# Block 2's attention scores from rounded high and low parts on all 128 rows, with the keys going through HBM

## The chip, the cores and the metric

The kernel runs on one core of one Trainium2 chip. The metric is the device time of one launch in microseconds (us). Before the change three runs took 877.80, 877.02 and 877.63 us, median 877.63.

The engines are TensorE (PE, matmuls; PEld is its weight load), VectorE (DVE), ScalarE (ACT), GpSimd (POOL) and SyncE (SP). SP computes nothing here: it issues most of the DMAs, one after the other, and its waits stand in the same line as its DMAs.

## The reference, cut to what matters

Two transformer blocks run one after the other on 256 tokens of width 1024. Block 2 has two attentions over 272 keys (256 tokens and 16 meta tokens): 16 heads that share 4 key heads in a window, and 8 differential heads with two parts each. Queries and keys are turned by their position (`rope`) before they meet:

```python
qa = rope(qa.reshape(B, Lp, SWA_Q_HEADS, HEAD_DIM), pos)      # 16 heads of 64
ka = rope(ka.reshape(B, Lp, SWA_KV_HEADS, HEAD_DIM), pos)     # 4 heads of 64
qb = rope(qb.reshape(B, Lp, DIFF_HEADS, 2, HEAD_DIM), pos)    # 8 heads, two parts
kb = rope(kb.reshape(B, Lp, DIFF_HEADS, 2, HEAD_DIM), pos)
# windowed attention, 16 heads
s_band = jnp.einsum('bqhgd,bkhd->bhgqk', qi, kb).astype(jnp.float32) * scale
# differential attention, 8 heads
s = jnp.einsum('bqhcd,bkhcd->bhcqk', qi, k).astype(jnp.float32) * scale + key_bias
p = jax.nn.softmax(s, axis=-1)
a = (p[:, :, 0] - lam * p[:, :, 1]).astype(v.dtype)
```

Everything is float32, and a head has 64 numbers per token.

## The kernel before

**Weights.** All weights come as 136 blobs of 128 x 2048 floats (1 MB). For each, SP loads `raw` (`load`, L721), ACT writes the rounded high part `whi` (`hi`, L783), DVE writes the rest `wlo` (`lo`, L1742), and PE multiplies with both. A product of two float32 matrices is thus three matmuls of rounded parts (`product`, L495 to L497). In block 2 the blobs go round three places in SBUF. I number the blobs of block 2's first part m = 0 to 33 (`m2` in the code).

**Steps.** The work of this part stands in steps q = 0 to 67, two for each blob: PE multiplies one half of blob q // 2 and then does what `slot(q)` lists. ACT and DVE have loops over the same q, with their own lists. Each engine works strictly in the order in which this is written, and only semaphores hold one back for another.

**Blobs.** Blobs 0 to 4 make keys, 5 and 8 to 11 values, 6, 7 and 12 to 17 queries. Then come gates and up-projections, the windowed ones (18 to 29, both kinds) before the differential ones (30 to 33 are the differential up-projection).

**A key blob.** PE writes it to a pair of PSUM banks; two pairs alternate, so blob m waits until blob m - 2 has been copied out (`wait_pair_free`, semaphores `taken_a` and `taken_d`). ACT copies it to `kraw` (`keys_out`, L1008); there are two of these too, so `keys_out(i)` first waits until key blob i - 2 has been turned (semaphore `kt_ok`). SP copies the halves of the heads across partitions to `kswap` with four DMAs (`swap_halves`, L759). DVE turns them: two products and a sum (`turned_keys`, L2231 to L2240), written straight to `ksT` and `kbT`. On DVE's list these turns stand ahead of the `lo` of a later blob. A query blob goes the same way (`queries_low` L1017, `queries_raw` L2212, `turned_queries` L2220 to L2224, into `qsT` and `qbT`); a value blob is copied out by ACT (`values_out`, L1026), turned over by PE (L1611) and copied again by ACT (`values_in`, L1035 to L1042).

**Units.** From step 22 on there is one unit for each step, 32 in all: two heads (or the two parts of one) for 128 tokens. PE computes its scores at the end of step 22 + U (L1639): one float32 matmul for each head, on 64 rows of the array, the first head on the upper 64 rows and the second on the lower 64. DVE takes the maximum (`unit_front`, L1941), ACT the exponentials (L1065), DVE the sums (`unit_back`), ACT scales (L1097), and two steps later PE transposes the result and multiplies it with the values. The scores of unit U wait for the maximum of unit U - 1 (`u_max`).

Of the kernel before, what the change touches and what calls it, by code (L numbers as in the profile page):

```python
# [18 lines left out]
F32 = mybir.dt.float32  # L19
# [5 lines left out]
P = 128  # L25
# [85 lines left out]
QUERIES = (6, 7, 12, 13, 14, 15, 16, 17)  # L111
# [3 lines left out]
VALUES_AT = {12: 0, 18: 1, 20: 2, 22: 3, 24: 4}  # L115
# [7 lines left out]
def values_blob(i):  # L123

    return 7 + i if i else 5
# [7 lines left out]
def unit_place(U):  # L133

    return U % S_UNITS // 8 * 4 + U % 4, U % 8 // 4


def query_made(U):

    cc, _ = unit_place(U)  # L140
    return 6 + U // S_UNITS * 4 + cc // 2
# [23 lines left out]
def build(nc, w, x, meta, consts, turns, rows, grow, out):  # L165

    with ExitStack() as ctx:
# [143 lines left out]
        o_tok = [at("o_tok0", [P, P], F32, dead + KC * TOK), new("o_tok1", [P, P]), new("o_tok2", [P, P])]  # L311
# [135 lines left out]
        def link(eng, name, ins):  # L447
# [12 lines left out]
            "aaaaa" + "a" + "dd" + "aaaa" + "dd" + "dddd" + "dddd" + "dd" + "dd")  # L460
# [255 lines left out]
        def _(sp):  # L716
# [58 lines left out]
        def _(act):  # L775
# [242 lines left out]

            def values_out(i):
# [25 lines left out]
            for q in range(2 * OUT2):  # L1045
# [221 lines left out]
        def _(pe):  # L1267
# [333 lines left out]
            def slot(q):  # L1601
# [26 lines left out]
                if 0 <= U < UNITS:  # L1628
                    cc, t = unit_place(U)
                    pe.wait_ge(kt_ok, query_made(U))  # L1630
# [4 lines left out]
                    qT = qsT if U < S_UNITS else qbT  # L1635
# [953 lines left out]
```

## Time and profile before

| | |
|---|---|
| median of three runs | 877.63 us |
| the profiled execution, and its span | 877.45 us, 875.6 us |
| PE busy | 868.0 us, 99% of the span, 4820 matmuls |
| DVE, ACT, POOL busy | 623.7 us (71%), 459.2 us (52%), 46.2 us (5%) |
| chain that ended last | PE 99% |
| DMA | 156.75 MB, mean 179 GB/s |

The profile is one execution. Of the 877.45 us the span covers 875.6, and 1.85 lie around it. Busy time of PE runs to the modelled end of each matmul, so that short pauses do not show as idle; the distance from the start of one matmul to the start of the next tells more. Block 2's first part lies between 396 and 655 us of the span, its key blobs between 396 and 427 us, and its units between 468 and 628 us.

### The profile page before, as it was taken

To read this page: it belongs to the slowest core of one execution; us is meant where nothing else is said; L and a number is where in the kernel's file an instruction comes from. 1 tells how busy PE (TensorE), PEld (TensorE's weight loads), DVE (VectorE), ACT (ScalarE), POOL (GpSimd) and SP (SyncE) were. 2 spreads that over 40 slices of the span, in tenths; PEclk is the share of its full clock that TensorE was granted. 3 is DMA by queue.
4 is the path that set the end of the run, shared out by engine and by line. 5 is a ranking of instruction groups with operands and counts; after the bars stand their busy time and mean duration, and the time that the engine had idled before them with its cause. 6 is when DMAs were issued, how large, how long until landed. Compare 5 with 4: busy or idle time off the path is not lost.

```text
span 875.6 us, 13035 instructions
## 1 busy us (share of the span) xinstructions
PE 868.0 (99%) x4820; PEld 731.3 (84%) x4820; DVE 623.7 (71%) x987; ACT 459.2 (52%) x735; POOL 46.2 (5%) x83
## 2 busy tenths in 40 slices
PE   9999999999999999999999999999999999999997
PEld 6887788888888888889998777777888888888886
DVE  6867777765876666668855888787766876666665
ACT  6546534334644444454556777677643654444443
POOL 1000010000200000002000000132300100000000
PEclk9999999999999999999999999999999999999999
DMA  9955344553565555353683335323274365555541
GB/s 328 412 207 187 129 160 144 192 192 144 190 242 190 189 195 188 142 190 104 207 300 106 123 123 170 145 100 142 97 265 175 119 228 189 183 192 192 186 143 48
DMA packets 26830, 156.75 MB, mean 179 GB/s; under 512 B 3600, under 2 KB 5136, under 8 KB 9376
## 3 DMA queue, kind: packets, MB, share of 16 engines
q1 hardware_dynamic: 24048, 148.71, 47.6%
q10 hardware_dynamic: 2736, 7.42, 2.4%
q8 instruction: 29, 0.48, 0.2%
q14 instruction: 17, 0.14, 0.0%
HBM read 151.45 MB, written 1.05 MB: 174 GB/s over the span
## 4 chain that ended last, share of the span: by engine, by line
PE 99%; DMA 0%; DVE 0%; DVEq 0%; SPq 0%; ACTq 0%; ACT 0%; issue 0%
PE ps L495 19%; PE ps L497 18%; PE ps L496 18%; PE ps L661 8%; PE ps L646 8%; PE ps L665 4%; PE ps L642 4%; PE ps L674 4%; PE ps L1639 2%; PE ps L676 2%; PE ps L530 1%; PE ps L1574 1%; PE ps L1598 1%; PE ps L1593 1%; PE ps L1588 1%; PE ps L1283 1%
## 5 line engine op out<-in xcount | busy, mean ns | idle before, releaser
L1742 DVE TENSOR_TENSOR wlo<-raw,whi 128x2048 fp32r<-128x2048 f32 x134 | 306.7, 2290 | 151.7 <-ACT whi L783 151.4
L783 ACT ACTIVATE whi<-raw 128x2048 fp32r<-128x2048 f32 x134 | 256.4, 1914 | 182.8 <-PE ps L497 110.8
L495 PE MATMUL ps<-whi,xT 128*128 128x512 f32 x192 | 76.8, 400 | 0.0
L497 PE MATMUL ps<-whi,xT 128*128 128x512 f32 x192 | 75.0, 391 | 0.0
L496 PE MATMUL ps<-wlo,xT 128*128 128x512 f32 x192 | 74.8, 390 | 0.0
L495 PE MATMUL ps<-whi,fT_h 128*128 128x512 f32 x128 | 50.2, 392 | 0.0
L496 PE MATMUL ps<-wlo,fT_h 128*128 128x512 f32 x128 | 49.8, 389 | 0.0
L497 PE MATMUL ps<-whi,fT_l 128*128 128x512 f32 x128 | 49.8, 389 | 0.0
L495 PE MATMUL ps<-x_all,whi 128*128 128x272 f32 x160 | 46.6, 291 | 0.0
L496 PE MATMUL ps<-x_all,whi 128*128 128x272 f32 x160 | 46.2, 289 | 0.0
L497 PE MATMUL ps<-x_all,wlo 128*128 128x272 f32 x160 | 46.2, 289 | 0.0
L497 PEld LDWEIGHTS ps<-whi,xT 128*128 128x128 f32 x192 | 36.0, 188 | 7.8
L1065 ACT ACTIVATE sc<-sc,usoft 128x272 f32<-128x272 f32 x64 | 32.7, 512 | 18.7 <-DVE usoft L1950 14.0
L495 PEld LDWEIGHTS ps<-whi,xT 128*128 128x128 f32 x192 | 36.1, 188 | 7.4
L646 PE MATMUL ps<-x_all,whi 128*128 128x512 f32 x176 | 42.0, 391 | 0.0
L496 PEld LDWEIGHTS ps<-wlo,xT 128*128 128x128 f32 x192 | 36.1, 188 | 7.0
L495 PE MATMUL ps<-whi,x_all 128*128 128x512 f32 x96 | 39.4, 410 | 0.0
L661 PE MATMUL ps<-x_all,whi 128*128 128x512 f32 x160 | 38.0, 390 | 0.0
L1224 POOL TENSOR_TENSOR stat<-stat,cst 128x1 f32<-128x1 f32 x10 | 11.9, 1204 | 490.0 <-DVE stat L1762 260.9
L646 PEld LDWEIGHTS ps<-x_all,whi 128*128 128x128 f32 x176 | 32.3, 188 | 6.3
L497 PE MATMUL ps<-whi,x_all 128*128 128x512 f32 x96 | 37.5, 391 | 0.0
L496 PE MATMUL ps<-wlo,x_all 128*128 128x512 f32 x96 | 37.4, 390 | 0.0
(347 smaller groups left out, 1834.5 us busy)
## 6 DMA issues: line engine op xcount, KB each, us to landing
raw<-weights SPq DMA_DIRECT2D x134, 1024.0 KB, 4.8
kswap<-kraw SPq DMA_DIRECT2D x52, 68.0 KB, 2.0
cst<-consts SPq DMA_DIRECT2D x1, 1371.0 KB, 13.0
raw<-weights SPq DMA_DIRECT2D x4, 256.0 KB, 5.5
raw<-weights SPq DMA_DIRECT2D x2, 512.0 KB, 7.2
gate_a<-gain_rows ACTq DMA_DIRECT2D x2, 512.0 KB, 7.7
gate_r<-gain_rows ACTq DMA_DIRECT2D x2, 512.0 KB, 6.7
gate_s<-gain_rows ACTq DMA_DIRECT2D x2, 512.0 KB, 6.6
```

The lines of the kernel that those rows point to most:

```text
L495: pe.matmul(o, lh, rh, start=first, stop=False)
L496: pe.matmul(o, lh, rl, start=False, stop=False)
L497: return pe.matmul(o, ll, rh, start=False, stop=last)
L642: pe.matmul(ps[:, bank0 + j, 0:TOK], vl[:, k, j * P:(j + 1) * P], x[:, 0, k, :], start=k == 0, stop=False, skip_group_check=True)
L646: m = pe.matmul(ps[:, bank0 + j, :], vh[:, k, j * P:(j + 1) * P], x[:, :, k, :], start=False, stop=k == KC - 1, skip_group_check=True)
L661: pe.matmul(ps[:, bank0 + j, :], vh[:, k, j * P:(j + 1) * P], x[:, :, k, :], start=k == 0, stop=False)
L665: m = pe.matmul(ps[:, bank0 + j, 0:TOK], vl[:, k, j * P:(j + 1) * P], x[:, 0, k, :], start=False, stop=k == KC - 1)
L674: pe.matmul(ps[:, bank + j, :], vh[:, k, j * P:(j + 1) * P], x2[:, :, k, :], start=k == 0, stop=False)
L676: m = pe.matmul(ps[:, bank + j, 0:TOK], vl[:, k, j * P:(j + 1) * P], x2[:, 0, k, :], start=False, stop=k == KC - 1)
L783: act.activation(whi[s][:], raw[s][:], ACT.Copy).then_inc(split_hi, 1)
L1065: ins = act.activation(scores(U, u), scores(U, u), ACT.Exp, bias=st[:, 2, u:u + 1], accum_out=st[:, 4, u:u + 1])
L1742: dve.tensor_tensor(wlo[s][:], raw[s][:], whi[s][:], ALU.subtract).then_inc(split_lo, 1)
```

## The change

The scores are computed from rounded parts as well. Queries and keys are each split into high (rounded) and low part. For one head the query's high part stands on 64 rows of the array and its low part on the other 64 (`qs`, `qd`), and the key comes in two forms, the high part on all 128 rows and the low part on all 128 rows (`kB`). Two matmuls of 128 rows then give (high + low) times high and (high + low) times low. A unit has four of them instead of two float32 ones.

To make the parts, ACT writes the high part and DVE the rest: `keys_high`, `keys_rest` for five key blobs, `queries_high`, `queries_rest` for eight query blobs. To bring the parts to their rows, SP stores the keys' parts in HBM (`store_keys`, 5 DMAs) and reads them back twice over into a ring of two chunks (`load_shared_keys`, 12 DMAs; `load_keys`, 8 times 4), and copies the queries' parts inside SBUF (`store_queries`, 8 times 4). `kt_ok` now counts the rests and no longer the turns; the turns have the new semaphore `rot_ok`. `keys_out(i)` waits for `kt_ok` as before.

Blobs are reordered: queries are 6, 7, 9, 10, 12, 13, 15, 17 and values 5, 8, 11, 14, 16; the windowed up-projection moves from 26 to 29 to 22 to 25. The two loads of gate rows on ACT move from steps 13 and 40 to steps 38 and 54, and the gates' steps on DVE and ACT with the blobs.

```diff
-QUERIES = (6, 7, 12, 13, 14, 15, 16, 17)
+QUERIES = (6, 7, 9, 10, 12, 13, 15, 17)
+QUERY_PLACE = (0, 1, 4, 2, 3, 5, 6, 7)
+VALUES = (5, 8, 11, 14, 16)
-VALUES_AT = {12: 0, 18: 1, 20: 2, 22: 3, 24: 4}
+VALUES_AT = {12: 0, 18: 1, 24: 2, 30: 3, 34: 4}
...
+            def store_keys(i):
+
+                sp.wait_ge(kt_ok, i + 1)
+                sp.dma_start(kd[i], knat[i % 2][:].bitcast(F32)).then_inc(kd_out[i % 2], 16)
+
+            def load_shared_keys(r):
+
+                if r == 0:
+                    sp.wait_ge(kd_out[0], 16 * 3)
+                    sp.wait_ge(kd_out[1], 16 * 2)
+                for copy in range(2):
+                    o = slice(copy * DH, (copy + 1) * DH)
+                    sp.dma_start(kB[r][o, 0:2, 0:KEYS], kd[0, 0:DH, :, r, :]).then_inc(kb_in[r], 16)
+                    sp.dma_start(kB[r][o, 2:4, N_META:KEYS], kd[0, DH:P, :, r, 0:TOK]).then_inc(kb_in[r], 16)
+                    sp.dma_start(kB[r][o, 2:4, 0:N_META], kd[0, DH:P, :, r, TOK:KEYS]).then_inc(kb_in[r], 16)
+
+            def load_keys(cc):
+
+                sp.wait_ge(u_sc, 2 * cc + 14 if cc else 8)
+                for u in range(2):
+                    for copy in range(2):
+                        sp.dma_start(kB[cc % 2][copy * DH:(copy + 1) * DH, 2 * u:2 * u + 2, 0:KEYS],
+                                     kd[1 + cc // 2, u * DH:(u + 1) * DH, :, cc % 2, :]).then_inc(kb_in[cc % 2], 16)
+
+            def store_queries(m2):
+
+                i = QUERIES.index(m2)
+                sp.wait_ge(kt_ok, 5 + i + 1)
...
+                sp.dma_start(dst[0][low, both, :], hi[low].bitcast(F32)).then_inc(q_in[j], 16)
+                sp.dma_start(dst[0][high, both, :], lo[low].bitcast(F32)).then_inc(q_in[j], 16)
+                sp.dma_start(dst[1][low, both, :], lo[high].bitcast(F32)).then_inc(q_in[j], 16)
+                sp.dma_start(dst[1][high, both, :], hi[high].bitcast(F32)).then_inc(q_in[j], 16)
+
-            plain = N1 + 24
+            plain = N1 + 30
             for n in range(N1, plain):
                 load(n, w[n], n - 2)
-                if n - N1 - 4 in SWAPPED:
-                    swap_halves(n - N1 - 4)
+                m = n - N1
+                if 7 <= m < 12:
+                    store_keys(m - 7)
+                if m in (12, 13):
+                    load_shared_keys(m - 12)
+                if m == 19:
+                    load_keys(0)
+                if 22 <= m < 29:
+                    load_keys(m - 21)
+                if m - 6 in QUERIES:
+                    store_queries(m - 6)
+                if m - 4 in SWAPPED:
+                    swap_halves(m - 4)
...
+            def keys_high(i):
+
+                act.wait_ge(rot_ok, i + 1)
+                if i >= 2:
+
+                    act.wait_ge(kd_out[i % 2], 16 * (i // 2))
+                act.activation(knat[i % 2][:, 0], kraw[i % 2][:], ACT.Copy).then_inc(rot_hi, 1)
+
+            def queries_high(m2):
+
+                i = QUERIES.index(m2)
+                act.wait_ge(rot_ok, 5 + i + 1)
+                if i >= 2:
+
+                    act.wait_ge(q_in[QUERY_PLACE[i - 2]], 64)
+                act.activation(qh[i % 2][:], kraw[m2 % 2][:, :, 0:TOK], ACT.Copy).then_inc(rot_hi, 1)
...
+                if q in (4, 6, 8, 10, 12):
+                    keys_high(q // 2 - 2)
+                if q % 2 == 1 and (q - 5) // 2 in QUERIES:
+                    queries_high((q - 5) // 2)
...
                 if 0 <= U < UNITS:
                     cc, t = unit_place(U)
-                    pe.wait_ge(kt_ok, query_made(U))
+                    if t == 0:
+                        pe.wait_ge(q_in[query_of(U)], 64)
+                        pe.wait_ge(kb_in[key_slot(U)], keys_loaded(U))
...
                     for u in range(2):
-                        half = slice(u * DH, (u + 1) * DH)
-                        kT = ksT[half, cc // 4, :] if U < S_UNITS else kbT[half, cc, :]
-                        m = pe.matmul(ps[:, 4 + u, 0:KEYS], qT[half, cc, t * P:(t + 1) * P], kT, start=True, stop=True)
+                        for v in range(2):
+                            m = pe.matmul(ps[:, 4 + u, 0:KEYS], qT[u][:, cc, t * P:(t + 1) * P].bitcast(F32R),
+                                          kT[:, 2 * u + v, 0:KEYS].bitcast(F32R), start=v == 0, stop=v == 1)
...
+            def queries_rest(m2):
+
+                i = QUERIES.index(m2)
+                dve.wait_ge(rot_hi, 5 + i + 1)
+                dve.tensor_tensor(ql[i % 2][:], kraw[m2 % 2][:, :, 0:TOK], qh[i % 2][:], ALU.subtract).then_inc(kt_ok, 1)
+
+            def keys_rest(i):
+
+                dve.wait_ge(rot_hi, i + 1)
+                dve.tensor_tensor(knat[i % 2][:, 1], kraw[i % 2][:], knat[i % 2][:, 0], ALU.subtract).then_inc(kt_ok, 1)
...
-                if i == 0:
-                    dve.tensor_tensor(ksT[0:DH], kraw[b][0:DH], kswap[b][0:DH], ALU.add)
...
-                m.then_inc(kt_ok, 1)
+                dve.tensor_tensor(kraw[b][:], kraw[b][:], kswap[b][:], ALU.add).then_inc(rot_ok, 1)
...
+                if q in (5, 7, 9, 11, 13):
+                    keys_rest((q - 5) // 2)
...
+                if q % 2 == 1 and (q - 5) // 2 in QUERIES:
+                    queries_rest((q - 5) // 2)
```

**ACT, from `keys_out(1)` in step 4 on.** Before; the number behind a name is the buffer's, `whi2` is the high part of blob 4 and `whi3` that of blob 5:

```order
L1008 ACTIVATE kraw1_118<-ps 128x272 x2
L783 ACTIVATE whi2_56<-raw2_55 128x2048
L1008 ACTIVATE kraw0_117<-ps 128x272 x2
L783 ACTIVATE whi3_59<-raw3_58 128x2048
L1008 ACTIVATE kraw1_118<-ps 128x272 x2
```

The same place of ACT in the changed kernel (`knat` holds a key blob's two parts):

```order
L1085 ACTIVATE kraw1_118<-ps 128x272 x2
L1102 ACTIVATE knat0_121<-kraw0_117 128x544
L860 ACTIVATE whi2_56<-raw2_55 128x2048
L1085 ACTIVATE kraw0_117<-ps 128x272 x2
L1102 ACTIVATE knat1_122<-kraw1_118 128x544
L860 ACTIVATE whi3_59<-raw3_58 128x2048
L1085 ACTIVATE kraw1_118<-ps 128x272 x2
```

A `keys_high` has come between each `keys_out` and the `hi` behind it, and it needs a turn that DVE has to finish.

**DVE, from `turned_keys(0)` in step 4 on.** Before; `wlo2` belongs to blob 4, `wlo3` to blob 5:

```order
L2231 TENSOR_TENSOR kraw0_117<-kraw0_117,turn_142 128x544
L2232 TENSOR_TENSOR kswap0_119<-kswap0_119,turn_142 128x544
L2234 TENSOR_TENSOR ksT_122<-kraw0_117,kswap0_119 64x544
L2235 TENSOR_TENSOR ksT_122<-kraw0_117,kswap0_119 64x2x256
L2237 TENSOR_TENSOR ksT_122<-kraw0_117,kswap0_119 64x2x16
L1742 TENSOR_TENSOR wlo2_57<-raw2_55,whi2_56 128x2048
L2231 TENSOR_TENSOR kraw1_118<-kraw1_118,turn_142 128x544
L2232 TENSOR_TENSOR kswap1_120<-kswap1_120,turn_142 128x544
L2240 TENSOR_TENSOR kbT_121<-kraw1_118,kswap1_120 128x544
```

The same place of DVE in the changed kernel:

```order
L2343 TENSOR_TENSOR kraw0_117<-kraw0_117,turn_149 128x544
L2344 TENSOR_TENSOR kswap0_119<-kswap0_119,turn_149 128x544
L2345 TENSOR_TENSOR kraw0_117<-kraw0_117,kswap0_119 128x544
L1844 TENSOR_TENSOR wlo2_57<-raw2_55,whi2_56 128x2048
L2343 TENSOR_TENSOR kraw1_118<-kraw1_118,turn_149 128x544
L2344 TENSOR_TENSOR kswap1_120<-kswap1_120,turn_149 128x544
L2345 TENSOR_TENSOR kraw1_118<-kraw1_118,kswap1_120 128x544
L2336 TENSOR_TENSOR knat0_121<-kraw0_117,knat0_121 128x544
```

`kt_ok` was raised for key blob 0 ahead of `wlo2` and is now raised behind the turn of key blob 1, by the rest (L2336).

**SP, from the load of blob 13 (`raw2`) to the swap of blob 10.** Before, the same stretch, blobs 12 to 16, had loads and one swap alone:

```order
L721 DMA raw1_52<-weights 128x2048
L721 DMA raw2_55<-weights 128x2048
L721 DMA raw3_58<-weights 128x2048
L721 DMA raw1_52<-weights 128x2048
L721 DMA raw2_55<-weights 128x2048
L759 DMA kswap0_119<-kraw0_117 32x544 x4
```

In the changed kernel, from the load of blob 13 on; `key_parts` is the HBM scratch:

```order
L750 DMA raw2_55<-weights 128x2048
L802 DMA kB1_124<-key_parts 64x2x272
L803 DMA kB1_124<-key_parts 64x2x256
L804 DMA kB1_124<-key_parts 64x2x16
L802 DMA kB1_124<-key_parts 64x2x272
L803 DMA kB1_124<-key_parts 64x2x256
L804 DMA kB1_124<-key_parts 64x2x16
L822 DMA qs0_137<-qh1_135 64x512
L823 DMA qs0_137<-ql1_153 64x512
L824 DMA qs1_138<-ql1_153 64x512
L825 DMA qs1_138<-qh1_135 64x512
L788 DMA kswap1_120<-kraw1_118 32x544 x4
```

The swap of blob 9 (the last row) stands behind ten new DMAs, and the ten of blob 12 stand ahead of those.

## Rows read from the trace of the kernel before

**Rows 1.** The page: busy time of the engines, and the chain by engine.

```profile
PE 868.0 (99%) x4820; PEld 731.3 (84%) x4820; DVE 623.7 (71%) x987; ACT 459.2 (52%) x735; POOL 46.2 (5%) x83
...
PE 99%; DMA 0%; DVE 0%; DVEq 0%; SPq 0%; ACTq 0%; ACT 0%; issue 0%
```

**Rows 2.** Timeline of PE at the scores of units 3 and 22: start, length, work.

```profile
481.54 0.73 PE L1639 MATMUL ps<-ksT,qsT 64*128 64x272 f32 x4
482.20 0.50 PE L674 MATMUL ps<-x_all,whi 128*128 128x512 f32 x1
...
574.45 0.27 PE L1577 MATMUL ps<-cst,sc 128*32 128x128 f32 x1
574.56 0.27 PE L1626 MATMUL ps<-cst,o_tok 128*128 128x128 f32 x1
574.76 0.73 PE L1639 MATMUL ps<-kbT,qbT 64*128 64x272 f32 x4
```

**Rows 3.** Timeline of PE in key blob 0: matmuls of rounded parts.

```profile
396.00 0.29 PE L496 MATMUL ps<-x_all,whi 128*128 128x272 f32 x1
396.13 0.29 PE L497 MATMUL ps<-x_all,wlo 128*128 128x272 f32 x1
```

**Rows 4.** Timeline of ACT, steps 4 to 14; in brackets idle time and its releaser.

```profile
408.55 0.69 ACT L1008 ACTIVATE kraw<-ps 128x272 f32<-128x272 f32 x2 [1.77 <-PE ps L497]
409.12 1.92 ACT L783 ACTIVATE whi<-raw 128x2048 fp32r<-128x2048 f32 x1
416.92 0.69 ACT L1008 ACTIVATE kraw<-ps 128x272 f32<-128x272 f32 x2 [5.88 <-DVE ksT L2237]
...
421.27 0.69 ACT L1008 ACTIVATE kraw<-ps 128x272 f32<-128x272 f32 x2 [1.86 <-DVE kbT L2240]
...
426.97 0.69 ACT L1008 ACTIVATE kraw<-ps 128x272 f32<-128x272 f32 x2 [3.21 <-PE ps L497]
...
433.05 0.62 ACT L1026 ACTIVATE kraw<-ps 128x544 f32<-128x544 f32 x1 [3.59 <-PE ps L497]
...
437.07 0.84 ACT L1042 ACTIVATE vs<-ps,stat 128x256 f32<-128x256 f32 x2
439.31 0.60 ACT L1017 ACTIVATE kraw<-ps 128x512 f32<-128x512 f32 x1 [1.40 <-PE ps L676]
```

**Rows 5.** Timeline of DVE, steps 4 to 11.

```profile
415.31 0.72 DVE L2234 TENSOR_TENSOR ksT<-kraw,kswap 64x544 f32<-64x544 f32 x1
...
416.86 2.29 DVE L1742 TENSOR_TENSOR wlo<-raw,whi 128x2048 fp32r<-128x2048 f32 x1
...
421.54 0.72 DVE L2231 TENSOR_TENSOR kraw<-kraw,turn 128x544 f32<-128x544 f32 x1 [0.36 <-DMA kswap<-kraw]
...
426.69 0.73 DVE L2231 TENSOR_TENSOR kraw<-kraw,turn 128x544 f32<-128x544 f32 x1 [0.82 <-DMA kswap<-kraw]
...
432.01 0.73 DVE L2231 TENSOR_TENSOR kraw<-kraw,turn 128x544 f32<-128x544 f32 x1 [0.99 <-DMA kswap<-kraw]
```

**Rows 6.** SP's timeline, one swap; all swaps' issue in ns; their landing.

```profile
417.63 2.41 SPq L759 DMA_DIRECT2D kswap<-kraw  x4
...
L759 SPq DMA_DIRECT2D kswap<-kraw x52: 507/591/1482, 403.2 to 538.4; - x52
...
DMA to landing us min/median/max: 1.9/2.0/3.9
```

**Rows 7.** Timelines: DVE at unit 0's scores, PE and DVE at unit 15's.

```profile
468.59 0.44 DVE L1941 CUSTOM_DVE_ANT_0 sc<-ps,cst 128x272 f32<-128x272 f32 x1 [6.26 <-PE ps L1639]
...
541.48 0.73 PE L1639 MATMUL ps<-ksT,qsT 64*128 64x272 f32 x4
...
543.91 0.43 DVE L1941 CUSTOM_DVE_ANT_0 sc<-ps,cst 128x272 f32<-128x272 f32 x1
```

**Rows 8.** Windows: length, busy PE, PEld, DVE, ACT, POOL; clock, DMA share, GB/s.

```profile
500.00:540.00 40.00, 40.00 (x291) 31.04 (x290) 35.79 (x100) 28.65 (x80) 0.00 (x0) 1.00 0.38 125
...
870.00:875.60 5.60, 0.00 (x0) 0.00 (x0) 2.69 (x5) 0.70 (x2) 0.55 (x1) 0.67 0.50 187
```

More of the change, by code:

```diff
@@ L123, in values_blob @@
 def values_blob(i):
-    return 7 + i if i else 5
+    return VALUES[i]
 def swaps_before(m2):
@@ L133, in unit_place, with query_of, key_slot, keys_loaded @@
 def unit_place(U):
-    return U % S_UNITS // 8 * 4 + U % 4, U % 8 // 4
-def query_made(U):
+    return U % S_UNITS // 2, U % 2
+def query_of(U):
     cc, _ = unit_place(U)
-    return 6 + U // S_UNITS * 4 + cc // 2
+    return U // S_UNITS * 4 + cc // 2
+def key_slot(U):
+    cc, _ = unit_place(U)
+    return cc // 4 if U < S_UNITS else cc % 2
+def keys_loaded(U):
+    cc, _ = unit_place(U)
+    return 96 if U < S_UNITS else 96 + 64 * (cc // 2 + 1)
 def slot_of(n):
@@ L285, in build @@
         kswap = [new("kswap0", [P, 2, KEYS]), new("kswap1", [P, 2, KEYS])]
-        kbT = new("kbT", [P, F_HEADS, KEYS])
-        ksT = new("ksT", [P, S_KV // 2, KEYS])
+        keys_at = top[0]
+        knat = [new("knat0", [P, 2, 2, KEYS], F32R), new("knat1", [P, 2, 2, KEYS], F32R)]
+        top[0] = keys_at
+        kB = [new("kB0", [P, 4, XSTEP]), new("kB1", [P, 4, XSTEP])]
         vs_meta = new("vs_meta", [P, S_KV * DH])
         o_junk = new("o_junk", [P, P])
-        rrow2 = new("rrow2", [P, TOK])
+        rrow2 = at("rrow2", [P, TOK], F32, top[0])
+        qh = [new("qh0", [P, 2, TOK], F32R)]
+        ql = [new("ql0", [P, 2, TOK], F32R)]
         assert top[0] <= 3 * BLOB
@@ L409, in build @@
         v_ps = sem("v_ps")
+        rot_ok = sem("rot_ok")
+        rot_hi = sem("rot_hi")
         kt_ok = sem("kt_ok")
+        kd_out = [sem("kd_out0"), sem("kd_out1")]
+        kb_in = [sem("kb_in0"), sem("kb_in1")]
+        q_in = [sem(f"q_in{j}") for j in range(len(QUERIES))]
         ql_ok = sem("ql_ok")
@@ new lines, in load_keys @@
+            def load_keys(cc):
[7 more added lines that the diff above has]
+                sp.wait_ge(kt_ok, 5 + i + 1)
+                j = QUERY_PLACE[i]
+                both = slice(2 * (j % 4), 2 * (j % 4) + 2)
+                hi, lo, dst = qh[i % 2], ql[i % 2], qs if j < 4 else qd
+                low, high = slice(0, DH), slice(DH, P)
+                sp.dma_start(dst[0][low, both, :], hi[low].bitcast(F32)).then_inc(q_in[j], 16)
+                sp.dma_start(dst[0][high, both, :], lo[low].bitcast(F32)).then_inc(q_in[j], 16)
+                sp.dma_start(dst[1][low, both, :], lo[high].bitcast(F32)).then_inc(q_in[j], 16)
+                sp.dma_start(dst[1][high, both, :], hi[high].bitcast(F32)).then_inc(q_in[j], 16)
@@ L2481, in weight_stream @@
     out += blob_tokens(w, at[2], 256)
-    for q in range(2):
-        out += blob_tokens(qa, 256 * q, 256)
-    for q in range(4):
-        out += blob_tokens(w, at[5] + 256 * q, 256)
-    for q in range(2, 4):
-        out += blob_tokens(qa, 256 * q, 256)
-    for q in range(4):
-        out += blob_tokens(w, at[3] + 256 * q, 256)
-    for q in range(4):
-        out += blob_tokens(w, at[6] + BANK * q)
-    for up in (head_pairs(np.asarray(i["w_branch_swa_2"])[0], 0, 0), np.asarray(i["w_branch_diff_2"])[0]):
+    values = 0
+    for m2 in range(6, 18):
+        if m2 in QUERIES:
+            j = QUERY_PLACE[QUERIES.index(m2)]
+            out += blob_tokens(qa, 256 * j, 256) if j < 4 else blob_tokens(w, at[3] + 256 * (j - 4), 256)
+        else:
+            out += blob_tokens(w, at[5] + 256 * values, 256)
+            values += 1
+    for g, up in enumerate((head_pairs(np.asarray(i["w_branch_swa_2"])[0], 0, 0), np.asarray(i["w_branch_diff_2"])[0])):
+        for q in range(2):
+            out += blob_tokens(w, at[6] + BANK * (2 * g + q))
         out += blob_tokens(up, 0) + blob_tokens(up, BANK)
```

50 lines of the change are left out of this document (25 added, 25 removed).

## The prediction, made before the changed kernel ran

> **What bounds the kernel now.** I read the page first: PE is busy for 99% of the span and the chain that ended last is 99% PE [rows 1], so whatever PE does not have to do is time saved, and whatever makes PE wait is time lost in full. Next I read PE's timeline at a unit's scores, for the price of what is removed [rows 2, 3]. Then the timelines of ACT, DVE and SP over the key blobs, because that is where the change adds waits: the reader is to see there how early each result is that PE needs [rows 4 to 6]. Last come the units, where DVE has the least spare time [rows 7, 8].
>
> Two kinds of lead matter. Around the key blobs ACT's copy of key blob 2 waited 5.88 us for DVE and was done at 416.92 + 0.69 = 417.6 [rows 4]; PE needed that bank for blob 4. Blob 4 ended at 426.97 and blob 1 at 408.55 [rows 4], 6.1 us for each, so blob 4 began at 420.8. The lead was 3.2 us. The low part of blob 4 was ready at 416.86 + 2.29 = 419.1 [rows 5], a lead of 1.7.
>
> **What the change saves.** Before, the four records of one unit's scores take PE from 481.54 to 482.20, 0.66 us [rows 2]. Matmuls of rounded parts with 272 columns start 0.125 us apart [rows 3] (two starts show 0.13 by rounding; I take 0.125), so the four new ones need 0.50: 0.16 saved in each of the 32 units. In the 16 differential units a step goes too: their scores come 0.20 behind the transpose ahead of them, where two transposes stand 0.11 apart [rows 2]. The new matmuls use all 128 rows as the transposes do, so I count 0.09 more for each. The windowed units come behind matmuls of 64 columns, and I count nothing there. Sum: 32 x 0.16 + 16 x 0.09 = 6.6 us. Bounds: 3.4 if a pause of 0.1 stays behind the scores in all units, 8.0 if all 32 lose the 0.09. I take 6.6, the value that changes only what rows 2 show.
>
> The Trainium skill (TensorEngine Tiling, Key Properties) says that changing the tiling mode, though not merely the tile, drains the engine. By that rule the windowed units, whose neighbours use another mode than full size, keep their pause, and the saving is 6.6; without it, with the 0.09 a matter of float32 alone, it would be 8.0. The 0.20 against 0.11 agrees with the rule and does not prove it.
>
> **The key blobs, where the new waits are.** The new ACT copy is priced as ACT's 128x544 copy, 0.6 (L1026 [rows 4]), the new DVE subtraction as a 544-wide sum, 0.7 [rows 5]; a turn is three of these, 2.1. Both have the shapes of the new work, only their sources differ. I follow the chain in the span's time.
>
> Step 4 and 5: the turn of key 0 ends at 415.31 + 0.7 = 416.0. ACT, free since 409.2, now stands at `keys_high(0)` and not at the high part of blob 4, so that part is made from 416.65 to 418.6 instead of 409.1 to 411.0. DVE then does the low part of blob 4 (to 420.85), the turn of key 1 (2.1, to 422.95) and only then the rest of key 0 (to 423.65). This raises `kt_ok`, for which `keys_out(2)` waits: copied out at 424.35 instead of 417.6. PE waits for the bank from 420.7: **3.65 us**.
>
> Step 7: from a copied key to its turn, SP's four issues (2.41) and the landing (2.0) [rows 6], it took 3.9, 4.7 and 4.35 us (417.6 to 421.54, 421.96 to 426.69, 427.66 to 432.01 [rows 4, 5]); I take 4.3. Turn of key 2 from 428.65 to 430.75, rest of key 1 to 431.4, low part of blob 5 to 433.65. PE ends blob 4 at 424.35 + 6.1 = 430.45: **3.2 us**.
>
> Step 9: `keys_out(3)` to 432.05, turn 436.35 to 438.45, rest of key 2 to 439.1, low part of blob 6 to 441.35. PE ends blob 5 at 439.75: **1.6 us**.
>
> Step 11 and 12: `keys_out(4)` to 439.8, turn 444.1 to 446.2, rest of key 3 to 446.85. `values_out(0)` needs this buffer, so the values are out at 447.45. PE comes to their transposes after half of blob 6. That blob took 433.05 to 439.31 [rows 4] with six transposes at 0.11, so 2.8 for a half: 444.15, **3.3 us**.
>
> Step 13: ACT goes on with `keys_high(4)`, a high part of 1.92 and the two kinds of value copies (0.84 for L1042 [rows 4] and an estimated 0.5 for the small one), to 451.4; PE would want that bank at 450.95: **0.45 us**.
>
> Sum 12.2 us. Blob 6 then ends at 451 instead of 439.3 (L1017 [rows 4]). With 3.9 or 4.7 for the swaps, three of which are on this chain, it is 11.0 or 13.4. `keys_high(2)` also waits until the store of key 0 has landed. No row shows a store to HBM; it is issued at about 427.5 and has until 437.8. Below, it costs nothing; above, if it took three times the slowest swap's landing (11.7 us [rows 6]), 1.4. I take 0. Past blob 7 DVE has no more key turns on its list and catches up.
>
> **SP's queue.** A DMA costs SP about 0.6 us (2.41 for four [rows 6]), and the change adds 81, 49 us of SP time. Most of it has cover, since the weights are loaded well ahead. At one place it has none: the swap of blob 9 stands behind 22 issues in SP's turns for blobs 12 and 13, 13 us. SP comes to the load of blob 12 at 461.7, after the swap of blob 7 (DVE reaches that query at 459.3: behind the low part of blob 7 at 449.1 stand two more low parts, each behind its high part, and two sums), and waits to 463.5 for the last store. Ten issues, a load and ten more put the swap at 476.2 to 478.6, landed at 480.5. The turn of blob 9 stands ahead of unit 0's maximum on DVE: 480.5 + 2.0 + 1.0 = 483.5. PE, from 451.4 on, does three query blobs (5.6), a value blob (6.1), transposes (0.65) and half of blob 11 (3.0), has these scores done at 478.5, and wants the maximum for the next at 481.6: 1.9 us. ACT's copy for the next values waits for the rest of blob 9 as well, another 0.8. I take 2.7. Bounds: with the quickest issue, 0.51 [rows 6], the swap is 1.8 earlier and 0.9 stays; at 0.7 it is 5.
>
> **DVE in the units.** In steps 28 to 37 DVE falls behind: at unit 0 it waits for the scores, at unit 15 it starts 543.91 - 541.48 = 2.4 us after PE began them [rows 7], and it is busy 35.79 of 40 us [rows 8]. The change makes PE's step 0.16 shorter there and adds a subtraction of about 0.6 for each query blob, but spreads the queries: 4.8 instead of 6 of them between steps 24 and 39, 4.8 x 3.1 us against 6 x 2.5 (a sum, a turn, and now the rest; estimates from rows 5), equal work in 16 x 0.16 = 2.5 us less. Before, no wait came of it; now it starts without a lead, as just worked out. I take 1.5, bounds 0 and 4 (the 2.5 and as much as one step of its 2.4 lag gives back). The gates' steps move with their blobs at the same distance and cost nothing; key and query reads (3 steps, 13 us ahead of use) neither.
>
> **Sum.** -6.6 + 12.2 + 2.7 + 1.5 = +9.8 us. The profiled execution took 877.45, which gives 887.3; it lies 0.2 below the median, so about 887.5.
>
> **The rivals.**
> 1. The new waits fit into the leads, and only the saving is left: 877.6 - 6.6 = 871. For it: the waits of ACT's copies for DVE shrink by themselves, 5.88, 1.86, and the third waits for PE instead [rows 4]. Against it: leads of 3.2 and 1.7 us stand against delays of 6.7 and 1.8. The point from which it decides is 6.6 us of stall: if the `kt_ok` of key 0 came before 420, half of the chain would be gone. A mixture can also end near zero.
> 2. SP becomes the bound: if the 20 new issues ahead of the swap of blob 9 cost 1.0 each, between the median 0.59 and the slowest 1.48 [rows 6], it comes 8 us later and PE waits for all of it: 895.5. For it: the new ones have twice as many rows and pieces. Against it: the median.
> 3. PE's clock falls in the stalls. It is granted in full throughout, and at 0.67 on average in the last 5.6 us, where PE has nothing to do [rows 8]: a stretch at the lower level of 1.2 GHz after PE went idle. An average of 0.67 means that some 3.7 of the 5.6 us were at half. If each of the three stalls over 3 us led to as much, with PE at work in it, it would add 3 x 1.9 = 5.6 us: 893. The Trainium skill (TensorE: Matmul & The Clock Gate, HAM oscillation) says that idle gaps between bursts throttle PE again.
>
> **How the numbers follow.** Forecast 0.70, and its own range is 883 to 892; rival 1 0.10, a mixture near zero 0.04, rival 2 0.10, rival 3 0.06. The range of 881 to 895 holds the forecast with both ends of the swaps, of SP and of DVE, and most of rivals 2 and 3, and leaves out rival 1. Under 0.2% (1.75 us) no difference can be told. Faster 0.10, same 0.04, slower 0.86.
>
> **What would show it.** In the profile after, the scores' line takes four matmuls 0.125 apart. PE has idle time, for which the page names DVE's low parts, ACT's copies of keys and values: five pauses of 3.65, 3.2, 1.6, 3.3 and 0.45 us before 452. `keys_out(2)` starts at about 423.7. Unit 0's maximum waits for a swap. I am wrong if PE reaches blob 7 before 445, or if the pauses are there but between 455 and 620 us PE loses more than 8 us.

## The result, and the profile after

The changed kernel takes 891.83 us (median of four runs, 890.81 to 892.91) against 877.33 for the kernel before, measured beside it. The ratio is 1.0166, with a 95% interval of 1.0148 to 1.0184: slower by 14.5 us. The prediction said 887.5, with a range of 881 to 895. The profiled execution after has a span of 890.7 us against 875.6.

The page after, engines and the chain by engine; it answers to [rows 1]:

```profile
PE 868.0 (97%) x4820; PEld 743.6 (83%) x4820; DVE 630.6 (71%) x998; ACT 464.8 (52%) x748; POOL 46.8 (5%) x83
...
PE 88%; DVE 3%; SPq 3%; DMA 3%; ACT 1%; issue 1%; POOL 1%; DVEq 0%; ACTq 0%
```

PE has the same number of matmul records and the same busy time, and the second is chance: with the new scores alone (run 1 below) it is busy for 859.4 us, and most of what lies between that and 868.0 is work at half clock. PE is no longer busy for 99% of the span but for 97%. The chain's share, 88% PE against 99%, says that there are waits and not what they cost: in run 8, which beats both kernels, it is 86%. The waits of PE say where they are (what PE waited for: us in total, times, longest; `usoft` holds the unit's maximum, `kraw` the copies of keys and values, `vs` the values as the units use them, `wlo` a low part of weights):

```profile
PE ps L1740 <- DVE usoft L2050: 4.9, 1, 4.9
PE ps L1711 <- ACT kraw L1120: 3.7, 1, 3.7
PE ps L524 <- ACT kraw L1085: 3.6, 1, 3.6
PE ps L1414 <- DVE kaT L2070: 1.4, 1, 1.4
PE ps L703 <- ACT vs L1136: 1.3, 1, 1.3
PE ps L703 <- DVE wlo L1844: 1.2, 1, 1.2
```

The fourth stands at the start of the kernel, before as after. The other five are new: scores of unit 1 (L1740), transposes of the first values (L1711), blob 4 (L524), blobs 7 and 6 (L703). PE's timeline shows the same, here at blob 4, blob 6, the end of blob 6's first half, blob 7 and unit 1:

```profile
423.66 0.56 PE L524 MATMUL ps<-x_all,whi 128*128 128x272 f32 x1 [3.58 <-ACT kraw L1085]
424.02 0.43 PE L525 MATMUL ps<-x_all,whi 128*128 128x272 f32 x1
424.25 0.43 PE L526 MATMUL ps<-x_all,wlo 128*128 128x272 f32 x1
...
439.89 2.11 PE L703 MATMUL ps<-x_all,whi 128*128 128x512 f32 x8 [1.16 <-DVE wlo L1844]
...
446.70 0.69 PE L1711 MATMUL ps<-cst,kraw 128*128 128x128 f32 x2 [3.75 <-ACT kraw L1120]
...
453.17 1.16 PE L703 MATMUL ps<-x_all,whi 128*128 128x512 f32 x4 [1.32 <-ACT vs L1136]
...
488.26 1.05 PE L1740 MATMUL ps<-kB,qs 128*128 128x272 f32 x3 [4.89 <-DVE usoft L2050]
```

Look at the second and third row too: behind the pause matmuls of 272 columns start 0.23 us apart, where [rows 3] has 0.125. The windows (length, busy PE, PEld, DVE, ACT, POOL; granted clock, DMA share, GB/s) show the reason: three stretches at 0.50, the lower level of 1.2 GHz, with PE at work in them.

```profile
422.60:429.40 6.80, 5.74 (x25) 5.77 (x26) 2.06 (x4) 3.02 (x4) 0.00 (x0) 0.50 0.46 106
429.40:446.50 17.10, 12.39 (x89) 11.45 (x87) 11.22 (x13) 6.78 (x9) 0.00 (x0) 1.00 0.79 246
446.50:449.90 3.40, 3.20 (x11) 2.67 (x12) 1.63 (x1) 0.76 (x3) 0.00 (x0) 0.50 0.74 239
...
487.40:494.20 6.80, 5.94 (x19) 5.18 (x20) 6.59 (x19) 4.24 (x14) 0.00 (x0) 0.50 0.79 269
494.20:640.00 145.80, 145.80 (x1012) 126.31 (x1010) 120.49 (x347) 107.94 (x303) 20.33 (x42) 1.00 0.60 187
```

**The key blobs.** ACT's timeline after, which answers to [rows 4]:

```profile
415.29 0.66 ACT L1102 ACTIVATE knat<-kraw 128x544 fp32r<-128x544 f32 x1 [6.82 <-DVE kraw L2345]
415.85 1.90 ACT L860 ACTIVATE whi<-raw 128x2048 fp32r<-128x2048 f32 x1
422.83 0.69 ACT L1085 ACTIVATE kraw<-ps 128x272 f32<-128x272 f32 x2 [5.08 <-DVE knat L2336]
...
430.29 0.69 ACT L1085 ACTIVATE kraw<-ps 128x272 f32<-128x272 f32 x2 [4.43 <-DVE knat L2336]
433.49 0.66 ACT L1102 ACTIVATE knat<-kraw 128x544 fp32r<-128x544 f32 x1 [2.52 <-DMA key_parts<-knat]
437.73 0.69 ACT L1085 ACTIVATE kraw<-ps 128x272 f32<-128x272 f32 x2 [1.77 <-DVE knat L2336]
440.93 0.66 ACT L1102 ACTIVATE knat<-kraw 128x544 fp32r<-128x544 f32 x1 [2.52 <-DMA key_parts<-knat]
...
446.02 0.62 ACT L1120 ACTIVATE kraw<-ps 128x544 f32<-128x544 f32 x1 [2.63 <-DVE knat L2336]
449.29 0.66 ACT L1102 ACTIVATE knat<-kraw 128x544 fp32r<-128x544 f32 x1 [2.64 <-DMA key_parts<-knat]
449.85 1.90 ACT L860 ACTIVATE whi<-raw 128x2048 fp32r<-128x2048 f32 x1
...
452.19 0.84 ACT L1136 ACTIVATE vs<-ps,stat 128x256 f32<-128x256 f32 x2
```

The chain starts in the first row: ACT stands 6.82 us at `keys_high(0)`, and the high part of blob 4, made at 409.12 in [rows 4], comes at 415.85. `keys_out(2)` starts at 422.83 instead of 416.92. The chain goes round through `keys_out`, SP's swap, DVE's turn and rest, and back to the next `keys_out`. Three times ACT also stands 2.5 to 2.6 us until the store of an earlier key blob has landed. The third time, at 449.29, a high part and the values' copies stand behind it, and PE's blob 7 (453.17) waits for the last of these copies.

From the page, DMA issues (us from issue to landing last):

```profile
raw<-weights SPq DMA_DIRECT2D x134, 1024.0 KB, 4.8
kB<-key_parts SPq DMA_DIRECT2D x36, 136.0 KB, 3.4
kswap<-kraw SPq DMA_DIRECT2D x52, 68.0 KB, 2.1
key_parts<-knat SPq DMA_DIRECT2D x5, 544.0 KB, 6.9
```

**Units 0 and 1.** SP (see [rows 6]), then DVE (see [rows 7]):

```profile
466.49 0.57 SPq L802 DMA_DIRECT2D kB<-key_parts  x1
...
480.23 0.60 SPq L825 DMA_DIRECT2D qs<-qh  x1
480.87 2.49 SPq L788 DMA_DIRECT2D kswap<-kraw  x4
```

```profile
485.07 0.69 DVE L2322 TENSOR_TENSOR kraw<-kraw,turn 128x512 f32<-128x512 f32 x1 [6.64 <-DMA kswap<-kraw]
...
487.01 0.43 DVE L2043 CUSTOM_DVE_ANT_0 sc<-ps,cst 128x272 f32<-128x272 f32 x1
```

The swap of blob 9 stands behind 21 issues, DVE waits 6.64 us for it ahead of unit 0's maximum, and PE's scores of unit 1 wait for that.

**The balance.** The first key blob starts 0.77 us earlier in the trace after (395.11 against 395.88), and up to the end of blob 3 this stays so. It isn't gained by the change: the distance is there after the first 9 us, in which both kernels do the same, and over the ten profiled executions of this document that start lies between 395.10 and 396.23. Counted from there, the end of blob 8 comes 14.9 us later, and the end of the kernel 15.8. Blobs 0 to 8 have the same content in both kernels, so 14.9 is the loss at the key blobs. From there to the end another 0.9 is lost: the pause of 5.05 and its stretch at half speed, less what the scores save.

### The profile page after: what moved, and what is told of

It is laid out like the page before. It is cut to its first block, busy times and chain, and to the rows that moved or that the text cites. A ratio compares the mean times of both kernels' runs of the same rounds, so it can differ in the third digit from the quotient of the medians.

```text
span 890.7 us, 13143 instructions
## 1 busy us (share of the span) xinstructions
PE 868.0 (97%) x4820; PEld 743.6 (83%) x4820; DVE 630.6 (71%) x998; ACT 464.8 (52%) x748; POOL 46.8 (5%) x83
## 4 chain that ended last, share of the span: by engine, by line
PE 88%; DVE 3%; SPq 3%; DMA 3%; ACT 1%; issue 1%; POOL 1%; DVEq 0%; ACTq 0%
PE ps L524 16%; PE ps L526 16%; PE ps L525 16%; PE ps L690 8%; PE ps L675 7%; PE ps L694 4%; PE ps L671 4%; PE ps L1740 2%; PE ps L703 2%; DMA key_parts<-knat 2%; PE ps L559 1%; SPq L788 1%; PE ps L1674 1%; PE ps L705 1%; PE ps L1698 1%
## 5 line engine op out<-in xcount | busy, mean ns | idle before, releaser
L524 PE MATMUL ps<-whi,xT 128*128 128x512 f32 x192 | 76.9, 400 | 0.0
L524 PE MATMUL ps<-x_all,whi 128*128 128x272 f32 x160 | 47.8, 299 | 3.6 <-ACT kraw L1085 3.6
L524 PE MATMUL ps<-whi,fT_h 128*128 128x512 f32 x128 | 50.3, 393 | 0.0
L525 PE MATMUL ps<-x_all,whi 128*128 128x272 f32 x160 | 47.3, 296 | 0.0
L524 PEld LDWEIGHTS ps<-whi,xT 128*128 128x128 f32 x192 | 36.1, 188 | 7.3
L524 PE MATMUL ps<-whi,x_all 128*128 128x512 f32 x96 | 38.2, 398 | 0.0
```

The lines of the kernel that those rows point to most:

```text
L524: pe.matmul(o, lh, rh, start=first, stop=False)
L525: pe.matmul(o, lh, rl, start=False, stop=False)
```

## The experiments

Each is a change to the kernel after, except the first. Ratios are to the kernel before, run beside it.

**1. The scores alone, in the kernel before.** Instead of the two float32 matmuls of a unit, four rounded ones on 128 rows, straight from the kernel's queries and keys; without the parts, so the scores are other numbers. The four tiles of queries and keys are declared as rounded (not shown).

```diff
+                    kT = ksT[:, cc // 4, :] if U < S_UNITS else kbT[:, cc, :]
                     for u in range(2):
-                        half = slice(u * DH, (u + 1) * DH)
-                        kT = ksT[half, cc // 4, :] if U < S_UNITS else kbT[half, cc, :]
-                        m = pe.matmul(ps[:, 4 + u, 0:KEYS], qT[half, cc, t * P:(t + 1) * P], kT, start=True, stop=True)
+                        for v in range(2):
+                            m = pe.matmul(ps[:, 4 + u, 0:KEYS], qT[:, cc, t * P:(t + 1) * P],
+                                          kT, start=v == 0, stop=v == 1)
```

> The kernel before with one thing changed: a unit's scores are four matmuls of rounded numbers on all 128 rows in place of two float32 ones on 64 rows each; no parts are made or moved, so the scores are not those of the reference. It prices the saving alone. My forecast priced it at 6.6 us (0.16 in each of 32 units, 0.09 more in the differential ones). The profile of the changed kernel suggests more: its undisturbed steps are 0.17 us shorter in the windowed units (5.00 to 4.83) and 0.36 in the differential ones (4.70 to 4.34), 8.5 us in all. By the first 870.7 us, by the second 868.8; the rival, that the saving was an effect of the reordered blobs, says 877.3.

870.52 us, ratio 0.9928 (0.9912 to 0.9945): 6.4 us saved. The forecast's 6.6 stands.

**2. Everything but the scores' form.** The kernel after with float32 scores on 64 rows, from the high parts alone.

```diff
-                        for v in range(2):
-                            m = pe.matmul(ps[:, 4 + u, 0:KEYS], qT[u][:, cc, t * P:(t + 1) * P].bitcast(F32R),
-                                          kT[:, 2 * u + v, 0:KEYS].bitcast(F32R), start=v == 0, stop=v == 1)
+                        half = slice(u * DH, (u + 1) * DH)
+                        m = pe.matmul(ps[:, 4 + u, 0:KEYS], qT[u][half, cc, t * P:(t + 1) * P],
+                                      kT[half, 2 * u, 0:KEYS], start=True, stop=True)
```

> The changed kernel with the scores computed as before, two float32 matmuls on 64 rows each, from the high parts alone (the low parts are made and moved but not used, so the scores are less exact). All making and moving of parts stays. It prices everything but the saving. If the loss lies in the making and moving, it is 8 us slower than the changed kernel, about 900, and shows the same pauses: some 3.6, 1.2, 3.7 and 1.3 us over the key blobs and nearly 5 at unit 1. If part of the loss came from the new scores themselves (reads of the ring, DVE too late because PE's steps are shorter), it is less than 8 slower, 895 or so.

899.26 us, ratio 1.0246 (1.0225 to 1.0266): 7.4 us above the kernel after, with the same pauses in the trace (3.86, 1.44, 4.16 and 4.37 us). From unit 2's scores to unit 31's, where neither kernel has a long pause, it takes 142.7 us for 136.3, 6.5 more. The saving is in the changed kernel too, and the loss is in what surrounds the scores.

**3. The key blobs in another order.** All the same work. ACT makes the high part of the weights ahead of `keys_high`, DVE makes the rest ahead of the next turn, SP's stores come one blob earlier.

```diff
# ACT, step q
-                if q in (4, 6, 8, 10, 12):
-                    keys_high(q // 2 - 2)
+                if q == 13:
+                    keys_high(4)
...
                     hi(N1 + m + 2)
+                if q in (4, 6, 8, 10):
+                    keys_high(q // 2 - 2)
...
# DVE: rest, lo, turn in the place of lo, turn, rest (in step 5 lo, rest, turn)
...
# SP
-                if 7 <= m < 12:
-                    store_keys(m - 7)
+                if 6 <= m < 11:
+                    store_keys(m - 6)
```

> The changed kernel with another order over the key blobs: ACT makes the weights' high part ahead of keys_high (the last keys_high goes behind the value copies), DVE makes a key's rest, and the next low part, ahead of the next key's turn, and SP stores a key one blob earlier, ahead of the next swap. No operation is taken away. If the pauses over the key blobs come from the places of these in their lists, kt_ok of key 0 comes at about 418.5 instead of 422.7, and of the 14.6 us lost between blob 3 and blob 7 at most 1 is left, with the clock at its upper level there: 877 to 880, with unit 1's pause still in it. If it is the amount of new work on ACT and DVE, or the landing of the stores (6.9 us each), that counts, most of the loss stays: 888 or more.

878.42 us (ten runs, 876.09 to 881.64), ratio 1.0017 (1.0004 to 1.0029): 13.4 us come back. The loss at the key blobs is order and not work. Three places changed at once, on ACT, DVE and SP, and no run tells what each is worth. PE's waits in this run:

```profile
PE ps L1742 <- DVE usoft L2052: 6.7, 1, 6.7
...
PE ps L1713 <- ACT kraw L1120: 0.8, 2, 0.4
```

The key blobs' waits shrank to 0.8 us, and the wait at unit 1 grew from 4.9 to 6.7: PE arrives earlier, and SP's row of issues is as long as it was. The profiled execution took 881.01, 2.6 us above this run's median, so the 6.7 may be more than the usual wait.

**4. The first swap ahead.** SP issues the swap of blob 9 ahead of the second block of key loads.

```diff
+                if m == 13:
+                    swap_halves(9)
...
-                if m - 4 in SWAPPED:
+                if m - 4 in SWAPPED and m != 13:
```

> The changed kernel with one swap moved: SP issues the swap of query blob 9 behind the load of blob 13, ahead of the six reads of keys and the four copies of query parts that stood before it. If unit 1's pause of 4.9 us is the SP queue ahead of that swap, the pause goes, the fall of the clock with it: 7 us less, 884.5 to 885.5. If DVE's own work is late there, or the copies only move the wait to the query parts, at most 2 us are gained: 890.

891.73 us, ratio 1.0162 (1.0145 to 1.0179): nothing. Unit 1's pause is gone, and one step later PE waits as long:

```profile
PE ps L1676 <- ACT sc L1197: 4.6, 1, 4.6
PE ps L1713 <- ACT kraw L1122: 3.8, 2, 3.7
```

The swap of blob 10 now stands behind the ten issues (it starts at 486.13), and DVE's turn of that blob stands ahead of unit 1's sums. My expectation missed this second swap.

**5. No swap behind the long row.** As in 4 (only the first ten issues and the load go ahead), and the second block of key loads two blobs later.

```diff
-                if m in (12, 13):
-                    load_shared_keys(m - 12)
+                if m in (12, 15):
+                    load_shared_keys((m - 12) // 3)
```

> The changed kernel with the second block of ten shared key loads issued by SP two blobs later (at blob 15 in the place of 13), and the swap of query blob 9 ahead of the store of queries in the same step. All swaps of queries then stand in front of SP's long block. With only the first swap put ahead, the pause had moved from unit 0's turn to unit 1's, behind the same ten issues. Theory (SP's 20 issues of 0.6 us in a row are what makes the units late): no pause over 1 us at unit 0, 1 or 2, no half clock between 480 and 500 us, and 4.9 us of pause with 2 to 2.5 us of clock come back: 884.5 to 885.5. Rival 1 (DVE's order at the first units costs a pause of its own): 1 to 5 us stay, 886 to 890. Rival 2 (the later block delays keys of later units): a new pause between 500 and 530 us, 890 or more.

887.56 us, ratio 1.0113 (1.0098 to 1.0129): 4.3 us back. Unit 1's pause is 1.9 us instead of 5.2, and the clock stays at 1.00 there:

```profile
480.00:500.00 20.00, 18.00 (x135) 15.72 (x133) 16.17 (x44) 14.09 (x34) 0.00 (x0) 1.00 0.91 253
```

The time lies in rival 1's range, and its reason does not show: the long row made the units late, and the 1.8 us of pause that stay come from the swap itself. DVE's turn of blob 9 waits for it and starts at 481.96, 3.5 us behind the end of the swap's issues, where it took 2.0 in run 4; why this swap landed late is open. The rest of what is missing to the 7 I expected is that with the clock up two smaller pauses of 0.65 and 0.85 us appear at 488 and 518 (L1713, ACT's copy of values), as in run 6.

**6. PE kept busy in two pauses.** Matmuls without use, 13 ahead of blob 4 and 20 ahead of unit 1's scores; the waits stay.

```diff
+            def filler(count):
+                for k in range(count):
+                    pe.matmul(ps[:, 6, :], x2_h[:, k % KC, 0:P], x_all[:, 0, 0:2, 0:TOK], start=True, stop=True)
```

> The changed kernel with matmuls that serve no result (512 columns, into a bank of their own) in PE's two longest pauses: 13 before blob 4, 20 before unit 1's scores. What PE waits for stays the same; only PE is busy meanwhile. Theory (the granted clock falls because PE stood idle, and the stretch at half speed behind the pause costs time of its own): the granted clock stays at its upper level at 422 and 487 us; blob 4 takes 6.1 us again in the place of 8.85, of which the wait behind it takes some back; behind unit 1's pause 2.5 to 3 us come back for good; 888 to 890. Rival 1 (the clock cost nothing that the waits would not have cost): 891.8. Rival 2 (the clock falls for another reason): it falls here too, 891.8 or more.

892.62 us, ratio 1.0173 (1.0159 to 1.0187): no gain, although the clock did what the theory says. Windows at blob 4, at the unfilled pause of blob 6, and behind unit 1's:

```profile
424.40:430.40 6.00, 6.00 (x48) 6.00 (x48) 2.18 (x4) 2.18 (x2) 0.00 (x0) 1.00 0.55 134
...
448.90:452.30 3.40, 3.40 (x12) 2.71 (x10) 1.08 (x2) 2.06 (x2) 0.00 (x0) 0.50 0.52 155
...
489.40:496.00 6.60, 6.18 (x39) 5.47 (x40) 6.43 (x16) 4.36 (x15) 0.00 (x0) 1.00 0.93 287
```

The clock stays up where PE was kept busy and falls at the pause that was not filled. But the time is not there to be had, as PE's waits show:

```profile
PE ps L1711 <- ACT kraw L1120: 5.0, 3, 4.1
PE ps L524 <- DVE wlo L1853: 2.6, 1, 2.6
```

Blob 4 takes 6.1 us again, and then PE waits 2.6 for the low part of blob 5. The pause that I had forecast at 3.2 was there all along: in the kernel after, blob 4 at half speed filled it (8.8 us for the blob). At unit 1, 2.0 us are won by the end of blob 12, and by blob 20 PE has waited 1.7 of them away for DVE and ACT in the units. The other runs agree at blob 4: from its first matmul to blob 5's it is 8.80 or 8.81 us in the kernel after and in runs 2, 4, 5, 6 and 7, with 6.8, 3.4 or no us of it at half clock. The unfilled pause of blob 6 has no such run, but a comparison: in run 2 the clock stays at 0.50 there to 453.1, in the kernel after to 449.9, and blob 7 starts 6.45 and 6.47 us behind the end of the pause. Blob 7 waits for ACT's copies either way. Rival 1 stands: the clock's fall cost almost nothing that the waits would not have cost.

**7. Five key buffers.** No `keys_high` waits for a store.

```diff
-                if i >= 2:
-
-                    act.wait_ge(kd_out[i % 2], 16 * (i // 2))
-                act.activation(knat[i % 2][:, 0], kraw[i % 2][:], ACT.Copy).then_inc(rot_hi, 1)
+                act.activation(knat[i][:, 0], kraw[i % 2][:], ACT.Copy).then_inc(rot_hi, 1)
...
```

> The changed kernel with five natural-key buffers in the place of two (three more tiles of float32, in the place of the scores' float32 tiles), so that keys_high of a step never waits for the 544 KB store that read the buffer before it. In the changed kernel keys_high stood 2.5 to 2.6 us three times for such a landing, and 2.1 us of the pause before blob 6 came out of that. Theory (the landing is a link in the chain before blobs 4, 6 and 8): the three waits go, the chain ACT - DVE - swap stays as it is, 1.5 to 3 us come back, 889 to 890.5. Rival (the landing is hidden behind the swap and DVE's turns, which are late anyway): 891.8, no change.

890.90 us, ratio 1.0155 (1.0141 to 1.0169). By the medians this is 0.9 us, less than the intervals can tell. The trace is clearer: ACT's three waits for a landing are gone, and with them PE's pause of 1.5 us ahead of blob 7. ACT's timeline at that place:

```profile
447.05 0.65 ACT L1102 ACTIVATE knat<-kraw 128x544 fp32r<-128x544 f32 x1
...
449.94 0.84 ACT L1136 ACTIVATE vs<-ps,stat 128x256 f32<-128x256 f32 x2
```

The values' copies start 2.25 us earlier than after, where they stood behind `keys_high(4)`. The pauses before blobs 4 and 6 are as they were: there the landing was hidden behind the swap. I had placed its effect at blob 6; it was at blob 7. There the landing and the slow stretch stand for each other: without the landing the copies are done at 450.8, and PE, at half clock, comes to blob 7 only at 452.27.

**8. The orders of 3 and 5 and the buffers of 7 together.**

> The three orders together: ACT's high parts ahead of the copies of keys and DVE's low parts ahead of the next turn (as in the run with the key order), SP's stores one blob earlier, five natural-key buffers, and SP's second block of shared keys at blob 15 behind the queries' swaps. All of the change's arithmetic stays. Theory (the change's loss is all order, and its matmuls are worth what the scores alone gave, 6.4 us): no pause of PE over 1 us anywhere between 415 and 530 us, clock at its upper level throughout, 870 to 872, faster than both kernels. Rival 1 (DVE's and ACT's added work costs something in the units also without a pause): 873 to 876. Rival 2 (the pause at unit 1 moves once more): 875 to 880.

872.66 us (872.27 to 873.07), ratio 0.9948 (0.9935 to 0.9962): faster than both kernels, by 4.5 us than before, and 19.2 faster than the kernel after, where runs 3, 5 and 7 gave 13.4, 4.3 and 0.9 one by one. PE's waits and the clock over the stretch in question:

```profile
PE ps L1715 <- ACT kraw L1122: 1.8, 4, 0.6
```

```profile
415.00:530.00 115.00, 113.13 (x845) 102.62 (x845) 93.48 (x197) 77.78 (x166) 0.00 (x0) 1.00 0.75 233
```

Four pauses are left, of 0.62 to 0.90 us from one matmul to the next (434.7, 453.2, 473.0, 502.8). It lands 0.7 above my range, and 2.1 above the scores alone: about 1.3 from the two pauses in the units, 0.5 from the key blobs, 0.4 between blobs 36 and 38. That is rival 1 in small: ACT's copies of values stand behind the scaling of a unit or the rest of a query.

## Why the prediction was right, and where its sizes were off

The direction, the places and the mechanism held: nearly all loss is in waits that the new order makes, first at the key blobs, then at SP's queue. The time is 4.3 us above the forecast and inside the range. A part of that closeness is luck: 1.5 us were added for DVE in the units, a wait that this trace doesn't have, and they cover a part of what the other terms lack. Term by term, by the traces:

| term | forecast | measured |
|---|---|---|
| scores | -6.6 | -6.6, as what the other rows leave of the sum (run 1 alone: -6.4) |
| key blobs | +12.2 | +14.9 |
| SP's queue, unit 1 | +2.7 | +5.05, and 2.1 of clock behind it |
| DVE in the units | +1.5 | 0 beside the clock's 2.1; 1.3 without it (run 8) |
| blobs 36 to 38 | 0 | +0.4 |
| sum | +9.8 | +15.8 from blob 3 on; 15.1 between the spans, since the trace after starts 0.77 ahead |

- **Scores.** The sum was right and its parts were not. A unit of before has three costs: 0.20 ahead, 0.66, and a first matmul behind it that takes 0.34 to the next instead of 0.22. [rows 2] shows that last as a length of 0.50; I didn't count it. After, a differential unit:

```profile
596.47 0.27 PE L1726 MATMUL ps<-cst,o_tok 128*128 128x128 f32 x1
596.50 0.75 PE L1740 MATMUL ps<-kB,qd 128*128 128x272 f32 x4
597.09 0.39 PE L524 MATMUL ps<-whi,sT_h 128*128 128x512 f32 x1
597.31 0.39 PE L525 MATMUL ps<-wlo,sT_h 128*128 128x512 f32 x1
```

  0.03 + 0.59 + 0.22 instead of 0.20 + 0.66 + 0.34: 0.36 saved, forecast 0.25. In the windowed units the 0.20 stays, the block takes 0.61, and 0.17 is saved: 0.05 in it and 0.12 behind it. The gross is 16 x 0.36 + 16 x 0.17 = 8.5. Some 2 us of it are not there: the steps behind the scores of units 16 and 17 are only 0.13 and 0.14 shorter than before and that behind unit 29 is not, and in run 1 there are three pauses of 0.5 to 0.7 us at 532, 542 and 552. The Trainium skill (TensorEngine Tiling, Key Properties) has a change of tiling mode drain the engine. The trace agrees: behind matmuls of 64 columns the new scores still come 0.20 later, behind full ones 0.03.
- **Key blobs.** Forecast pauses 3.65, 3.2, 1.6, 3.3, 0.45. Measured, less the usual step: 3.75; none, but blob 4 longer by 2.75 at half speed in its place; 1.3; 3.9; and in the place of the 0.45 a pause of 1.5 ahead of blob 7, behind a half blob 6 that took 5.0 us with its transposes at half clock, where run 8 has 3.5. That is 14.7, and the rest of the 14.9 is spread over the steps. The first four are right within 0.6 each, and their errors cancel. The size that was wrong is blob 7's: 3.0 for 0.45. Its term is the landing of the stores, taken as 0 with an upper end of 1.4. A store landed after 6.9 us, against the 2.0 of a swap, from whose rows I bounded it; `keys_high(4)` waits 2.64 for it, and the values' copies behind it are done at 453.0 and not at the 451.4 of the forecast. Without the landing 1.5 come back (run 7), and the rest is then the clock's. `keys_out(2)` was forecast at 423.7 and came at 422.83, or 423.6 with the 0.77. Run 3 shows that the order alone makes this term: 13.4 us are back with the same instructions.
- **SP's queue.** Right place, right swap; the size was half. SP was free at 463.5, as forecast for the start of its row, but stood until 466.49 for the landing of the last store, issued at 458.94. Its 21 issues took 14.4 us and not 12.7: most stand 0.64 apart and not 0.6, and two took 1.05 and 1.13. So the swap came 4.7 later than forecast, and PE, held up at the key blobs, wanted unit 1's scores only 1.6 later (483.2 for 481.6): 1.9 + 3.1 = 5.0. The landing of a store, mis-sized above, is the larger part here too, 3.0 of the 4.7. The 0.8 that I had added for the next values does not show beside this pause. With the 2.1 of clock PE lost about 7.2 us here, close to the 8 that I had named as a sign of being wrong. This is a part of rival 2: not 1.0 for each issue, but 0.68.
- **Rival 3, the clock,** was a mechanism that did happen, in all three long pauses. In the traces PE's work became longer by 2.75, 1.55 and 2.1 us by it; the rival had 1.9 for each. But the rival adds it to the waits, and it mostly took the place of one: at blob 4 all of it did (run 6 and the 8.80 us of the other runs), ahead of blob 7 all of it by the comparison with run 2, and at unit 1 all but about 0.3 (run 6).
- **DVE in the units.** The 1.5 turned up as about 1.3, but only where the clock did not fall. It shows as ACT's late copies of values, in run 6 and in run 8, and behind these stands DVE: in run 8 the copy at 473.01 follows a scaling that waits 1.26 us for DVE's sums, and the one at 503.01 waits 0.52 us for the rest of a query.
- **Blobs 36 to 38.** 0.4 us go there in every kernel with the new parts, and not in run 1; PE waits 0.2 of it for DVE at L1383. The rest was not looked into.

## What to carry to other kernels

When an engine with an in-order list gets a new instruction that waits for another engine, the instruction costs little and what stands behind it pays: write the work that is already ready ahead of it. Here this, on ACT and DVE and with SP's stores one blob earlier, is worth 13 us, twice what the new matmuls save. A late swap or load is found by walking the issuing queue to its end: with one swap moved ahead of the row the wait sat down on the next, and only the row's own move took most of it away, 3.3 of 5.2 us. And waits, slow stretches and late engines in one place are alternatives and not terms of a sum, so take them away together before judging one. Losses in different places did add up: 18.6 us one by one, 19.2 together.

## What was not expected of the hardware

- A store of 544 KB to HBM (`key_parts`) landed 6.9 us after its issue, a load of 1024 KB after 4.8 (page after), and in the eight kernels that have this store the median is 6.1 to 7.1. Not every store is slow: the four of 256 KB that write the result (`y<-h`) landed after 2.2. Why is open.
- The granted clock fell to half in or just after each of the 16 pauses of PE from 3.8 to 7.0 us in these runs, and after none of 2.85 us or less. It stayed there for 3.4 us or about 6.8, at the same place for either in different runs (blob 4: 6.8 in the kernel after, 3.4 in runs 4, 5 and 7); what decides between them is open.
- The kernels with long pauses scatter more: ten runs of number 3 span 5.6 us, five of number 8 span 0.8. The lengths of the slow stretches may be the reason; with one profile for each this is not shown.
